# Order and shape of the small fp32 matmuls in the RWKV chunk steps x, y and state of a two-block transformer kernel

## The reference

```
def step(state, inp):
    r_t, w_t, k_t, v_t, a_t, b_t = inp
    sa = einsum('bhij,bhj->bhi', state, a_t)
    state = state * w_t + sa x b_t + v_t x k_t
    return state, einsum('bhij,bhj->bhi', state, r_t)
```

## Time and profile before

| | |
|---|---|
| median of 3 runs | 2194.01 us (2192.86 to 2194.59) |
| the profiled execution | 2192.86 us |
| its span, first to last instruction | 2190.8 us |
| granted TensorE clock, mean | 1.000 of full speed |
| TensorE matmul records | 16476, busy 2159.7 us |
| VectorE busy | 1678.0 us |
| ScalarE busy | 1266.2 us |

### The profile page before, as it was taken

The page is one execution under the profiler, slowest core; times in us unless marked ns, Lnnn a source line. Parts: engine busy times, 40 slices in busy tenths (PEclk is TensorE's granted clock), DMA queues, the critical chain, the costliest instruction groups (busy, mean ns, idle before and its releaser), DMA issues.

```text
span 2190.8 us, 39551 instructions
## 1 busy us (share of the span) xinstructions
PE 2159.7 (99%) x16476; PEld 1972.7 (90%) x16476; DVE 1678.0 (77%) x2609; ACT 1266.2 (58%) x2098; POOL 12.5 (1%) x20
## 2 busy tenths in 40 slices
PE   7999999999999999999999999999999999999999
PEld 6898989998998898998888999988898889998888
DVE  7877579887885769876787678888678766878875
ACT  4755456554755555555555457665565645676554
POOL 0000000000000000000000000000000000000000
PEclk9999999999999999999999999999999999999999
DMA  9554556777645347655555533565555554345553
GB/s 373 178 183 164 184 188 230 251 252 267 231 152 177 136 160 236 223 175 189 180 188 190 183 126 116 186 203 190 191 175 192 191 185 144 116 164 202 192 186 131
DMA packets 116229, 415.15 MB, mean 189 GB/s; under 512 B 13090, under 2 KB 16290, under 8 KB 115539
## 3 DMA queue, kind: packets, MB, share of 16 engines
q1 hardware_dynamic: 116050, 412.63, 55.8%
HBM read 409.42 MB, written 3.16 MB: 188 GB/s over the span
## 4 chain that ended last, share of the span: by engine, by line
PE 91%; DVE 5%; ACT 2%; DMA 1%; issue 0%; SPq 0%; ACTq 0%; DVEq 0%
PE bank L198 90%; DVE arena L205 2%; DVE lo L205 1%; ACT arena L250 1%; PE bank L202 1%; DMA raw<-W 1%; DVE arena L213 1%; DVE ada L222 0%; ACT hi L250 0%; DVE sml L225 0%; DMA xT<-x 0%; ACT L242 0%; ACT L250 0%; DVE h L205 0%; DVE h L213 0%
## 5 line engine op out<-in xcount | busy, mean ns | idle before, releaser
L198 PE MATMUL bank<-h,hi 128*128 128x256 f32 (+1 forms) x5344 | 1223.4, 314 | 0.0
L250 ACT ACTIVATE hi<-raw 128x1024 fp32r<-128x1024 f32 x656 | 689.1, 1056 | 593.3 <-PE bank L198 543.0
L198 PE MATMUL bank<-h,lo 128*128 128x256 f32 x3440 | 988.8, 287 | 5.0 <-DVE h L205 4.8
L198 PEld LDWEIGHTS bank<-h,hi 128*128 128x128 f32 x5344 | 881.2, 191 | 66.5 <-issue 2.6
L205 DVE TENSOR_TENSOR lo<-raw,hi 128x1024 fp32r<-128x1024 f32 x656 | 795.0, 1223 | 91.6 <-ACT hi L250 90.4
L198 PEld LDWEIGHTS bank<-h,lo 128*128 128x128 f32 x3440 | 655.3, 190 | 16.7 <-DVE h L205 6.1
L198 PE MATMUL bank<-act,hi 128*128 128x512 f32 x1056 | 370.0, 393 | 0.0
L198 PE MATMUL bank<-act,lo 128*128 128x256 f32 x1056 | 295.2, 280 | 0.0
L198 PEld LDWEIGHTS bank<-act,hi 128*128 128x128 f32 x1056 | 198.1, 188 | 46.7
L198 PE MATMUL bank<-arena 64*64 64x64 f32 (+6 forms) x3058 | 202.3, 259 | 6.0 <-DVE arena L205 4.4
L198 PEld LDWEIGHTS bank<-act,lo 128*128 128x128 f32 x1056 | 197.9, 187 | 0.0
(11 more groups left out here) (150 smaller groups left out, 1911.3 us busy)
## 6 DMA issues: line engine op xcount, KB each, us to landing
raw<-W SPq DMA_DIRECT2D x664, 512.0 KB, 3.4
ada<-WA SPq DMA_DIRECT2D x80, 512.0 KB, 3.9
arena<-WA SPq DMA_DIRECT2D x16, 512.0 KB, 14.5
p_projected<-arena SPq DMA_DIRECT2D x2, 1024.0 KB, 7.4
arena<-scr SPq DMA_DIRECT2D x16, 128.0 KB, 4.8
arena<-p_projected SPq DMA_DIRECT2D x2, 1024.0 KB, 4.8
xT<-x SPq DMA_DIRECT2D x2, 512.0 KB, 5.6
arena<-lora SPq DMA_DIRECT2D x2, 512.0 KB, 10.4
```

The costliest lines, as they stand in the source:

```text
L198: return self.done(lambda e: e.matmul(out, l, r, start=start, stop=stop, skip_group_check=True))
L250: return self.done(lambda e: e.activation(out, in_, f, scale=scale, **kw))
```

## The change

In `x` the two 128*64 matmuls of a head become one of 128*128 (all 128 tokens as weight columns, 64 moving columns). In chunk 1 the S1 matmul of a head, which has form 64*128, stands directly ahead of its NK matmul, which has form 128*128, where before all eight S1 matmuls came first. The two banks of `x` are taken one by one. In `y` and `state` the order becomes head by head: the two 128*64 matmuls of one head follow each other, and then come those of the next head; in chunk 1 each head's 64*64 matmul with S1 comes right after them, where before all eight stood in front. The flags that start and end the accumulation follow the new order. The sums are the same.

```diff
-                    outs = [take(GEN, ("x", l, c, g)) for g in range(2)]
-                    pe.wait_ge(v_rw, ("cross", l, c, 1, "K", 1))
-                    pe.wait_ge(a_rw, ("tok", l, "V", c))
-                    if c:
-                        pe.wait_ge(v_rw, ("state", l))
+                    for g in range(2):
+                        o = take(GEN, ("x", l, c, g))
+                        pe.wait_ge(v_rw, ("cross", l, c, 1, "K", 1))
+                        pe.wait_ge(a_rw, ("tok", l, "V", c))
+                        if c:
+                            pe.wait_ge(v_rw, ("state", l))
                         for m in range(4):
-                            for g in range(2):
-                                rows = slice(64 * g, 64 * g + 64)
-                                pe.mm(outs[g][:, m * 64:(m + 1) * 64], AR[rows, 2 * m + c, 0, :],
-                                      S1[rows, m * 64:(m + 1) * 64], m == 0, False)
-                    for g in range(2):
-                        for m in range(4):
-                            h = 2 * m + g
-                            for t in range(2):
-                                part = slice(64 * t, 64 * t + 64)
-                                i = pe.mm(outs[g][part, m * 64:(m + 1) * 64], NK[:, h, part], VT[:, h * 64:(h + 1) * 64],
-                                          c == 0, True)
+                            po, h = 64 * g, 2 * m + g
+                            om = o[:, m * 64:(m + 1) * 64]
+                            if c:
+                                pe.mm(om, AR[po:po + 64, 2 * m + c, 0, :], S1[po:po + 64, m * 64:(m + 1) * 64], True, False)
+                            i = pe.mm(om, NK[:, h, 0:128], VT[:, h * 64:(h + 1) * 64], c == 0, True)
                         i.then_inc(pe_rw, ("x", l, c, g))
...
-                        if c:
-                            for h in range(8):
-                                rows, m = slice(64 * (h % 2), 64 * (h % 2) + 64), h // 2
-                                pe.mm(o[rows, m * 128:(m + 1) * 128], S1[rows, m * 64:(m + 1) * 64],
-                                      AR[rows, 2 * m + c, 1, :], m == 0, False)
-                        for m in range(4):
-                            oh = [o[64 * g:64 * g + 64, m * 128:(m + 1) * 128] for g in range(2)]
-                            for g in range(2):
-                                h = 2 * m + g
-                                pe.mm(oh[g], Um[:, h * 64:(h + 1) * 64], NB[:, h, 128:256], c == 0, False)
-                            for g in range(2):
-                                h = 2 * m + g
-                                i = pe.mm(oh[g], VT[:, h * 64:(h + 1) * 64], NK[:, h, 128:256], False, True)
+                        for h in range(8):
+                            po, m = 64 * (h % 2), h // 2
+                            oh = o[po:po + 64, m * 128:(m + 1) * 128]
+                            pe.mm(oh, Um[:, h * 64:(h + 1) * 64], NB[:, h, 128:256], True, False)
+                            i = pe.mm(oh, VT[:, h * 64:(h + 1) * 64], NK[:, h, 128:256], False, c == 0)
+                            if c:
+                                i = pe.mm(oh, S1[po:po + 64, m * 64:(m + 1) * 64], AR[po:po + 64, 2 * m + c, 1, :], False, True)
                         i.then_inc(pe_rw, ("y", l, c))
...
-                            for m in range(4):
-                                oh = [o[64 * g:64 * g + 64, m * 64:(m + 1) * 64] for g in range(2)]
-                                for g in range(2):
-                                    cols = slice((2 * m + g) * 64, (2 * m + g + 1) * 64)
-                                    pe.mm(oh[g], tokB[:, cols], Um[:, cols], True, False)
-                                for g in range(2):
-                                    cols = slice((2 * m + g) * 64, (2 * m + g + 1) * 64)
-                                    i = pe.mm(oh[g], tokK[:, cols], VT[:, cols], False, True)
+                            for h in range(8):
+                                po, m = 64 * (h % 2), h // 2
+                                oh = o[po:po + 64, m * 64:(m + 1) * 64]
+                                pe.mm(oh, tokB[:, h * 64:(h + 1) * 64], Um[:, h * 64:(h + 1) * 64], True, False)
+                                i = pe.mm(oh, tokK[:, h * 64:(h + 1) * 64], VT[:, h * 64:(h + 1) * 64], False, True)
                             i.then_inc(pe_rw, ("state", l))
```

## The result

The changed kernel takes 2216.32 us (median, 2216.17 to 2217.41) against 2194.27 for the kernel before: +22.05 us, ratio 1.0101, interval 1.0089 to 1.0113. The forecast was 2209.8, in a range of 2202 to 2214. The direction is right. The size is not: the cost is 6.2 us above the forecast's sum of 15.8, and the time 6.5 us above the forecast time and outside the range.

A forecast was written before the change was run, and what follows sets the result against it. TensorE, busy 99% of the span, was taken to bound the kernel. Terms 1.36 + 4.8 + 9.2 + 0.4 = 15.8 us on 2192.86 gave 2208.7; with the median 1.15 above that execution, 2209.8 us, range 2202 to 2214.

The forecast's parts named there:

- The clock is no rival: TensorE's granted clock: stays at 1.00, the 2.4 GHz level, throughout, so no time was forecast for it.
- x, c = 0: Step x, chunk 0: sixteen unpartnered records at 0.11 us, 1.97 us for 1.29; +0.68 a layer, +1.36 in all.
- the one-column row: Profile row of records with one moving column, 0.117 us apart; basis for 0.11 us per record with 128 weight columns.
- x, c = 1: Step x, chunk 1: two shape changes a head, 5.76 us for 2.12; +3.64 a layer, +4.8 in all after cover.
- The cover behind it: Waits behind x of chunk 1 absorb delay: layer 0 pays 1.6 us of 3.64, layer 1 pays 3.2.
- y, c = 1: Step y, chunk 1: 0.94 us a head, 7.52 for 2.92; +4.60 a layer, +9.2 in all, nothing hides it.
- y, c = 0, and state: Step y of chunk 0 and step state: reordered halves cost +0.2 us a layer for both, 0.4 in all.
- Rival B: In y and state the column halves keep strict order: 2.9 in place of 0.4, +18.3 us, 2212.3; chance 0.18.
- the forecast's working for strict order: y of chunk 0: a run of four records takes 0.34 us instead of 0.22; eight runs, +0.93 us.
- Rival A: Shape changes in x and y cost nothing within a head: +7.6 us, 2201.6; chance 0.12.
- rival C: Tiles of different shape run side by side in x and y: not slower, −1.3 us, 2192.7; chance 0.06.

The follow-up runs named there:

- E1: Only x in its new form, y and state as in the kernel before; 2207.12 us, +12.65, ratio 1.0057 against the kernel before.
- E7: New x alone, each chunk 1 NK matmul followed by an unread one with 256 moving columns; 2208.24 us, +13.7, ratio 1.0060 against the kernel before.
- E4: Kernel before with only the order of column halves in y and state changed, S1 matmuls still in front; 2193.51 us, −0.96, ratio 0.9996.
- E11: Whole change except that x's chunk 1 S1 matmuls stay in front in one group; 2205.39 us, +11.8, ratio 1.0051 against the kernel before.
- E3: Kernel before with only x's merged 128*128 matmuls, chunk 1 S1 matmuls all first; 2196.63 us, +2.16, ratio 1.0008.
- E12: Changed kernel plus an unread 256-column matmul behind each NK matmul in x of chunk 1; 2216.06 us, +22.5, ratio 1.0097 against the kernel before.
- E2: Only y and state in their new order, x as in the kernel before; 2202.48 us, +8.0, ratio 1.0039 against the kernel before.
- E10: Kernel before with x's eight chunk 1 S1 matmuls of 64*128 split into sixteen of 64*64; 2194.53 us, +0.94, ratio 1.0002.

## Why the prediction was right in direction and wrong in size

- **The step that failed** is "The clock is no rival: with TensorE busy 2.97 of 8 us and 4.56 of 7 it stayed at 1.00". Stretches in which TensorE waits didn't lower the clock in that trace; the alternation of small matmuls in x of chunk 1 does, with TensorE shown busy all the time. The clock halves for 3.4 to 10.2 us just when main matmuls follow. The forecast had nothing for this. The changed kernel's trace has 4.4 us for it, that of E1 (5.63 + 6.04 = 11.7 for the same two steps, less 4.4) has 7.2, against 6.2 that are missing between the medians. How these 6.2 divide between x and stretches near the start isn't shown.
- **x, c = 0:** +0.66 measured, +0.68 forecast. The new form is paced by its 128 columns of weights, 0.11 us a record, as the one-column row said.
- **x, c = 1:** 5.81 us measured at full clock for 5.76 (layer 1). The cover behind it was right to 0.3 us: 1.3 and 3.2 for 1.6 and 3.2, from E7.
- **y, c = 1:** +4.60 a layer, as forecast.
- **y, c = 0, and state:** about +0.05 a layer in the trace of E4 and of the changed kernel, for +0.2 taken. Rival B is out. The measurement differs here from the Trainium skill ("TensorE: Matmul & The Clock Gate", Part 3, "What overlaps and what doesn't"), which has matmuls go strictly in order: y's 32 records are busy 2.0 us in E4 as before, where the forecast's working for strict order has 0.9 more.
- **Rival A** (free changes) and **rival C** are out: each change stands in the timeline at its price.
- **The base:** the profiled execution before had no stretch at half clock near the start, the one after had 6.8 us of it. Its main stream is 128.40 − 125.50 = 2.9 us late before the first changed step. With 1.3 for x of chunk 0, 8.8 for that of chunk 1, 9.2 and 0.1 for y and state this makes 22.3 of the 23.1 us between the two spans. The remaining 0.8 arise at one wait for VectorE behind the last changed step, here before and after:

```profile
834.89 0.39 PE L198 MATMUL bank<-h,lo 128*128 128x256 f32 x1 [0.92 <-DVE h L205]
...
857.72 0.39 PE L198 MATMUL bank<-h,lo 128*128 128x256 f32 x1 [1.39 <-DVE h L205]
```

- **Open:** what exactly lowers the clock. Four changes did it in one layer and not in the other, one change (E11) did it once and in E3's trace not at all. Why the wait at 857.72 grows is open too: main work is 22.0 us late ahead of it and 22.8 behind it in the changed kernel, in E3's trace 1.75 and 2.9, and E12's trace loses nothing there. The medians of E1 and E2 add up to +20.7 where the whole change has +22.05; their intervals are about 3 us wide to each side, so this gap may be noise.

## What to carry to other kernels

Keep small matmuls of one shape together, and let neighbours alternate between tiles of that shape: here a head by itself cost 0.73 us in x and 0.94 in y where the grouped order took 0.27 and 0.37. When a change makes TensorE change shape often, forecast the granted clock too: here it fell with TensorE's row at 100% busy (5.20 of 5.20 us ahead of the fall in layer 0), and of the 4.4 us that it cost, only 0.4 (6.23 − 5.81) came within x and the rest in the dense work behind. Read the mean granted clock first when a result is larger than its parts.

## What the runs showed of the hardware that was not expected

- The granted clock fell to 0.50 (1.2 GHz) within, or right behind, x with its alternating small matmuls, 3.3 to 5.8 us after its first one and with no idle time shown (changed kernel, E1), for 3.4, 6.8 or 10.2 us; 16 more records of 256 columns in between kept it at 1.00 (E7, E12), and it also stayed at 1.00 through y's alternation of 7.5 us (E2).
- Two column halves ran side by side with four records queued on one before the other's first: 2.0 us busy for 32 records either way (E4).
- Four 64*64 tiles ran at once: 32 records in 0.7 us (E10).
- At half clock the small 64*64 records stretch as well as the main ones: the step behind x took 1.97 us for 1.15.
